# An ordering model's prices for GpSimd, crossbar transposes and weight casts, and the first batch's state scalings, in a bidirectional gated-attention block

## The chip, the cores and the metric

The kernel runs on all 8 NeuronCores of one Trainium2 chip. Each core computes 4 of the 32 sequences alone; nothing passes between cores. The metric is the device time of the slowest core, in microseconds (us). In this text PE is TensorE (matmuls), DVE is VectorE, ACT is ScalarE, POOL is GpSimd and SP is SyncE, which here issues nearly all DMAs.

## What is computed

One encoder block on x of shape (32, 2048, 1024), with 16 learned meta tokens put ahead of each sequence and dropped at the end:

```python
u = rms_norm(concat(meta, x), g_pre)
(c_b, c_c, c_x, c_z, q, k, v, r, lr_f, lr_b, m_a, m_b) = split(u @ w_in)
y_conv = c_b * conv3(c_c * c_x, conv_w) * silu(c_z)          # centred, depthwise
g_f = log_sigmoid(lr_f @ w_gate_f + b_f) / 16                # and g_b, per head and key channel
o = gla(q, k, v, g_f, j <= t) + reversed_gla(q, k, v, g_b, j > t)   # 4 heads, key 128, value 256
#   per chunk: o = mask(q_in k_in^T) v + q_in @ state ; state = state * decay + k_dec^T v
y_gla = rms_norm_per_head(o) * silu(r)
merged = sigmoid(m_a) * (y_conv @ w_out_c) + sigmoid(m_b) * (y_gla @ w_out_g)
out = x + rms_norm(merged @ w_out, g_post)
```

Inputs and output are float32; the kernel's matmuls are bf16 with float32 accumulation.

## The kernel before

A core goes through its 4 sequences ("batches" in the code, numbered 0 to 3) one after the other. For each, 16 tiles of 128 positions are normalised, transposed and kept as `uT`; then come the projections of the 4 heads (k, q, v and the gates), the chunked attention forward and backward over 16 chunks of 128 positions, the short convolution channel group by channel group, four output products done by a seven-product scheme for 2x2 blocks (`stage6`), and the last projection with norm and residual (`stage7`). All of it is written as small items in chains (`put`), each with the items it comes after.

**A list scheduler sets the order.** While the program is built, `ListScheduler.run` takes at each point the item that would keep PE waiting least, by a model: `Sched.add` gives each instruction a start (its engine free, its operands ready, 0.2 us more across engines) and an end from a booked cost, and each DMA an end from one shared transfer time of bytes / 300 GB/s plus 2 us. The model alone sets the order of the instructions on each of the five queues; on the chip every engine then runs its queue strictly in that order and waits on semaphores. A booked cost that is changed thus changes no instruction by itself, but can move any of them, in all batches.

**Booked costs.** `ecost` (line 512) prices tensor operations on POOL and DVE; `dtr` (551) is a crossbar-transposing DMA, issued on SP; the weights of batch 0 are loaded by POOL's casting DMA (float32 to bf16, line 616) and written back as bf16 to `wsc`, from which SP loads them later.

**The state scalings.** The attention's state per head is a 128 x 256 float32 tile, `TF` forward and `TB` backward. For each chunk DVE adds the chunk's product to the decayed state (`stt`, line 522, reads PSUM), and the state times the decay is written as bf16: forward into a part of `GR` (`f_P`, line 956), backward into `SB` (`b_P`, line 1000). This scaling goes through `evac`, which picks among the engines it is given the one that the model has done first. A batch has 64 forward and 60 backward ones. The backward pass of a head is 8 items `b_O`, each for two chunks: six 128 x 256 matmuls (five in the first) from `SM`, `GR` and `SB`; ahead of them stand the two `KT` products of `b_P` and the four 128 x 128 score products of `b_S`. Below, a **step** is what PE has to do from the last matmul of one `b_O` to the last of the next, seven to a head.

**What batch 0 has besides.** x tiles 8 to 15 are transposed on the crossbar, the weights are cast and written back, and POOL prepares the sums of the 2x2 scheme's weights (`prep`, 32 times: two casts and four 256-column operations, tile `OS` or `ycX`). In the profile all matmuls have line 492, all ACT work line 509; DVE and POOL tensor-tensor work is line 518, scalings and other tensor-scalar work line 527, casts and copies 536.

Of the kernel before, what the change touches and what calls it, by code (L numbers as in the profile page):

```python
# [40 lines left out]
BLK_OFF = {}  # L41
# [310 lines left out]
def build_program(NB):  # L352
    nc = bass.Bass("TRN2", target_bir_lowering=False, dynamic_dma_scratch_size=2048)

    def din(name, shape, dt=F32):
        return nc.dram_tensor(name, list(shape), dt, kind="ExternalInput").ap()
# [3 lines left out]
    w_d = din("w_all", [W_TOTAL // 256, 256])  # L360
# [65 lines left out]
    def program(S):  # L426

        G = {"st": 0, "held": ()}
# [8 lines left out]
        def free_n(ap):  # L437
            n = 1
            for d in ap.shape[1:]:
                n *= d  # L440
            return n

        def narrow(*aps):
            return all(a.dtype in (BF16, U16) for a in aps)
# [46 lines left out]
        def mm(out, lhsT, rhs, start, stop, r, w, share=1, skip=False):  # L491
            S.add("pe", lambda e: e.matmul(out, lhsT=lhsT, rhs=rhs, start=start, stop=stop, skip_group_check=skip), r, w,  # L492
                  cost=max(0.025, free_n(rhs) / 2400.0 + 0.0025) / share)
# [17 lines left out]

        def ecost(eng, n, fast):
            if eng == "pool":
                return 0.15 + 2.17e-3 * n
            return 0.15 + (0.52e-3 if fast else 1.04e-3) * n

        def tt(eng, out, a, b, op, r, w):
# [20 lines left out]
        def evac(out, in_, r, w, scale=None, engs=("act", "dve")):  # L538

            n = free_n(out)  # L540
            cost = {"act": 0.17 + 0.82e-3 * n, "dve": ecost("dve", n, narrow(out, in_)), "pool": 0.2 + 1.15e-3 * n}
            eng = min(engs, key=lambda e: max(S.free[e], S.free["pe"]) + cost[e])
            cp(eng, out, in_, r, w, scale)
# [4 lines left out]
        def dma(q, out, in_, r, w, semkey, nbytes):  # L548
            return S.add(q, lambda e: e.dma_start(out=out, in_=in_), r, w, semkey=semkey, nbytes=nbytes)  # L549

        def dtr(out, in_, r, w, semkey, nbytes):
            S.add("sp", lambda e: e.dma_start(out=out, in_=in_, transpose=True), r, w, semkey=semkey, nbytes=nbytes, hold=1.1)  # L552

        def rot(name, bufs):
            i = G.get(("rot", name), 0)
# [9 lines left out]
        def wsrc(t, blk):  # L565
            off, cols, _ = BLK_OFF[blk]
            return t[off // 256:(off + 128 * cols) // 256, :].rearrange("(p a) n -> p (a n)", p=128)

        class WPool:
# [26 lines left out]
            def load(self, n):  # L596
                blk, kind, first = self.seq[n]
                own = G["wf", self.region]
                best = None
                for i, b in enumerate(self.kinds[kind]):  # L600
                    t = [own[u] for u in self.units(b)]
                    if None not in t and (best is None or max(t) < best[0]):
                        best = (max(t), i, b)
                if best is None:
                    raise NotReady()
                _, s, b = best
                G["wf", self.region] = tuple(None if u in self.units(b) else t for u, t in enumerate(own))
                G["ws", self.name, n] = b
                ap, k = self.ap(n)
                if kind in "ab":  # L610
                    _, g, p = blk
                    lo, hi = (0, 2048) if kind == "a" else (2048, 3584)
                    dma("sp", ap, wst_d[g * 4 + p, :, lo:hi], [("wst", g, p, z, kind) for z in range(2)], k,
                        ("w", kind, s), 256 * (hi - lo))
                elif first:
                    dma("pool", ap, wsrc(w_d, blk), [], k, ("wc", self.name, s), 512 * BLK_OFF[blk][1])
                else:
                    dma("sp", ap, wsrc(wsc_d, blk), [("wsc", blk)], k, ("w", self.name, s), 256 * BLK_OFF[blk][1])

# [320 lines left out]

        def f_init(hd, b):

            i_ap, i_k = TF[1](F32)
            if b > 0:
                dma("sp", i_ap, smeta_d[hd], [("smeta", hd)], i_k, ("tf",), 1 << 17)
            G["fT"] = 1
            G["fd"] = None
# [6 lines left out]
        def f_P(H, pr, t):  # L954
            bank, bk = nps()
            for z in range(2):
                i = pr * 2 + z
                k_ap, k_k = KTf[t](BF16, (i % 4) * 128, 128)
                v_ap, v_k = H.v(i)
                mm(bank[:, z * 256:(z + 1) * 256], k_ap, v_ap, True, True, k_k + v_k, bk)  # L960
            for z in range(2):
                i = pr * 2 + z
                old, oldk = TF[G["fT"]](F32)
                new, newk = TF[1 - G["fT"]](F32)
                s_ap, s_k = H.Sf(i)
                if G["fd"] is None:
                    evac(s_ap, old, oldk, s_k, engs=("act", "pool"))
                    tt("dve", new, bank[:, z * 256:(z + 1) * 256], old, ALU.add, bk + oldk, newk)
                else:
                    dc, dk = G["fd"]  # L970
                    evac(s_ap, old, oldk + dk, s_k, scale=dc, engs=("act", "pool", "dve"))
                    stt(new, old, dc, bank[:, z * 256:(z + 1) * 256], ALU.mult, ALU.add, oldk + dk + bk, newk)
                G["fT"] = 1 - G["fT"]
                G["fd"] = (H.dc(0, i), H.dk)
# [21 lines left out]
        def b_P(H, u):  # L996
            if u == 0:
                G["bd"] = None
                G["bT"] = 0
            n1 = 7 - 2 * (u % 4)  # L1000
            bank, bk = nps()
            nz = 1 if u == 7 else 2
            for z in range(nz):
                k_ap, k_k = KTb[u % 2](BF16, (1 - z) * 128, 128)
                v_ap, v_k = H.v(n1 - z)
                mm(bank[:, z * 256:(z + 1) * 256], k_ap, v_ap, True, True, k_k + v_k, bk)
            for z in range(nz):
                old, oldk = TB[G["bT"]](F32)
                new, newk = TB[1 - G["bT"]](F32)
                if G["bd"] is None:  # L1010
                    cp("dve", new, bank[:, 0:256], bk, newk)
                else:
                    dc, dk = G["bd"]
                    stt(new, old, dc, bank[:, z * 256:(z + 1) * 256], ALU.mult, ALU.add, oldk + dk + bk, newk)
                G["bT"] = 1 - G["bT"]
                G["bd"] = (H.dc(1, n1 - z), H.dk)
                s_ap, s_k = SBs[(u * 2 + z + 1) % 5](BF16)
                dc, dk = G["bd"]
                evac(s_ap, new, newk + dk, s_k, scale=dc, engs=("act", "pool", "dve"))

        def b_O(H, u):
            n1 = 7 - 2 * (u % 4)
# [575 lines left out]
        for z in range(4):  # L1598
            ap = REG["onT"][:, 2 * z * 2048:2 * z * 2048 + 4096].rearrange("p (r t) -> p r t", r=2)[:, :, 0:1024].bitcast(F32)
            keys = onT[2 * z](BF16, 0, 1024)[1] + onT[2 * z + 1](BF16, 0, 1024)[1]  # L1600
            xnext.append((ap, keys, True))
        for z in range(2):
            ap, keys = e1(F32, z * 1024, 1024)
# [95 lines left out]
    S = Sched()  # L1699
# [105 lines left out]
```

How the kernel before makes its waits and increments, by code:

```python
    def emit(self, eng, e, sems):  # L211
        waited = {}
        for op in self.ops[eng]:
            need = {}
            for d in op.deps:
                s, v = d.sig
                if v > need.get(s, 0):
                    need[s] = v
            for s, v in need.items():
                if waited.get(s, 0) >= v:
                    continue
                e.wait_ge(sems[s], v)
                waited[s] = v
            if op.fn is None:
                continue
            ins = op.fn(e)
            if op.semkey is not None:
                ins.then_inc(sems[op.sig[0]], 16)
            elif op.need:
                ins.then_inc(sems[op.sig[0]], 1)
```

## Time and profile before

| | |
|---|---|
| three runs | 2964.33, 2966.95, 2987.33 us (median 2966.95) |
| profiled execution | 2960.34 us; span of the slowest core 2958.8 us |
| spans of the 8 cores | 2949.3 to 2958.8 us, granted clock 0.983 to 0.987 |
| busy: PE, DVE, ACT, POOL | 2811.1, 1970.0, 1547.8, 1065.0 us |

The profile is of core 3, the slowest. PE is busy for 95% of the span, so 148 us are left in which it has no matmul. The granted clock is the share of full speed that the chip allows PE; a PE that is slowed shows as longer matmuls, not as idle time.

### The profile page before, as it was taken

The page shows a single profiled execution, that of the slowest core. Times are in us where ns is not written, and L with a number is a line of the kernel's source. Part 1 is how long each engine was busy: PE and PEld are TensorE (multiplying, and loading weights), DVE is VectorE, ACT ScalarE, POOL GpSimd, SP SyncE. Part 2 cuts the span into 40 slices and gives each one's busy share as a digit, 9 for nine tenths or more (in the row PEclk, how much of TensorE's full clock was granted, in tenths as well). Part 3 has the DMA queues.
Part 4 walks back from the last instruction along what each step waited for, and adds up shares of the span by engine and source line. Part 5 has one row for each costly group of instructions (what it writes and reads, how often), then busy time and mean ns, then how long its engine had stood idle before and what let it go on. Part 6 is the DMA issues. An engine that isn't in the chain of part 4 may idle for free.

```text
span 2958.8 us, 54281 instructions; the slowest of 8 cores (2949.3 to 2958.8 us)
## 1 busy us (share of the span) xinstructions
PE 2811.1 (95%) x15740; PEld 1475.3 (50%) x15740; DVE 1970.0 (67%) x2889; ACT 1547.8 (52%) x2921; POOL 1065.0 (36%) x1447
## 2 busy tenths in 40 slices
PE   6898897999999999999999999999999999999998
PEld 4555443444456665444445665444445656544443
DVE  5556676566677786567666778557667778656665
ACT  5556664433466764443456776343346776443243
POOL 4566565232232343125143334125323234312412
PEclk9999998999999999999999999999999999999999
DMA  9997755494553223376473322349456222334445
GB/s 226 186 179 170 170 156 151 153 269 147 181 165 74 74 65 110 127 220 176 150 208 100 79 66 72 112 153 261 137 183 168 74 74 64 110 115 151 137 137 169
DMA packets 370976, 423.01 MB, mean 143 GB/s; under 512 B 220528, under 2 KB 252272, under 8 KB 370176
## 3 DMA queue, kind: packets, MB, share of 16 engines
q1 hardware_dynamic: 361760, 402.56, 47.3%
q0 software_dynamic: 8928, 16.98, 4.3%
q8 instruction: 135, 2.21, 0.3%
q14 instruction: 153, 1.25, 0.1%
HBM read 324.65 MB, written 65.60 MB: 132 GB/s over the span
## 4 chain that ended last, share of the span: by engine, by line
PE 78%; DMA 7%; SPq 4%; issue 3%; DVE 3%; POOL 3%; ACT 2%; POOLq 0%; DVEq 0%; ACTq 0%
PE ps L492 78%; SPq L552 3%; POOL sb_OS L518 1%; SPq L549 1%; DMA wsc<-sb_W 1%; DMA wst<-sb_OS 1%; DMA sb_KT<-sb_GR 1%; DMA sb_ycT<-x 1%; DMA sb_W<-wst 1%; DMA sb_uT<-sb_ycX 1%; DMA sb_onT<-sb_ON 1%; DMA sb_onT<-x 0%; DMA sb_uT<-sb_ycT 0%; DVE sb_GR L518 0%; POOL sb_ycT L518 0%
## 5 line engine op out<-in xcount | busy, mean ns | idle before, releaser
L492 PE MATMUL ps<-sb_uT,sb_W 128*128 128x512 bf16 (+3 forms) x7680 | 1608.5, 370 | 22.0 <-DMA sb_uT<-sb_ycX 7.5
L492 PEld LDWEIGHTS ps<-sb_uT,sb_W 128*128 128x128 bf16 (+1 forms) x7680 | 728.6, 98 | 780.9 <-issue 66.1
L509 ACT ACTIVATE sb_CS<-ps 128x512 f32<-128x512 f32 (+3 forms) x544 | 304.5, 569 | 285.7 <-PE ps L492 273.6
L518 POOL TENSOR_TENSOR sb_GR<-sb_CS 128x512 bf16<-128x512 f32 x128 | 166.5, 1303 | 659.8 <-DVE sb_CS L522 654.4
L492 PE MATMUL ps<-sb_GR 128*128 128x512 bf16 (+2 forms) x1792 | 350.8, 319 | 9.2 <-DVE sb_GR L518 4.1
L492 PE MATMUL ps<-sb_GR,sb_W 128*128 128x512 bf16 x1072 | 264.9, 381 | 6.7 <-ACT sb_LR L509 5.9
L522 DVE SCALAR_TENSOR_TENSOR sb_CS<-sb_CS,sb_convw 128x512 f32<-128x512 bf16 x256 | 247.2, 974 | 17.0 <-ACT sb_CS L509 6.3
L518 DVE TENSOR_TENSOR sb_CS<-ps,sb_CS 128x512 f32<-128x512 f32 (+3 forms) x288 | 181.2, 629 | 115.7 <-PE ps L492 81.0
L492 PEld LDWEIGHTS ps<-sb_GR 128*128 128x128 bf16 x1792 | 164.2, 98 | 149.4 <-issue 14.1
L492 PE MATMUL ps<-sb_W,sb_uT 128*128 128x256 bf16 x2048 | 234.9, 273 | 1.1 <-ACT sb_MT L509 0.9
L518 POOL TENSOR_TENSOR sb_CS<-sb_CS 128x512 f32<-128x512 f32 x128 | 168.2, 1317 | 167.1 <-DVE sb_CS L522 101.9
L492 PEld LDWEIGHTS ps<-sb_W,sb_uT 128*128 128x128 bf16 x2048 | 198.9, 98 | 32.3 <-issue 3.0
L699 POOL TENSOR_TENSOR sb_stat<-sb_stat,sb_cst 128x2 f32<-128x2 f32 (+2 forms) x257 | 183.0, 712 | 38.5 <-POOL sb_stat L527 0.9
L901 DVE TENSOR_TENSOR_SCAN sb_AT<-sb_smask,sb_AT 128x1024 f32<-128x1024 bf16 x64 | 149.2, 2364 | 41.5 <-ACT sb_AT L509 41.5
L527 POOL TENSOR_SCALAR sb_SB<-sb_TB,sb_dcol 128x256 bf16<-128x256 f32 x125 | 63.0, 504 | 304.7 <-DVE sb_TB L522 155.5
L492 PEld LDWEIGHTS ps<-sb_GR,sb_W 128*128 128x128 bf16 x1072 | 104.7, 98 | 135.6 <-issue 12.5
L527 POOL TENSOR_SCALAR sb_GR<-sb_TF,sb_dcol 128x256 bf16<-128x256 f32 x143 | 78.7, 551 | 252.6 <-DVE sb_TF L522 185.9
L527 POOL TENSOR_SCALAR sb_stat<-sb_stat 128x2 f32<-128x2 f32 (+2 forms) x257 | 78.4, 305 | 236.7 <-ACT sb_TB L509 143.4
L509 ACT ACTIVATE sb_SM<-ps 128x256 bf16<-128x256 f32 x384 | 144.5, 378 | 35.3 <-PE ps L492 20.3
L509 ACT ACTIVATE sb_TB<-ps 128x1024 bf16<-128x1024 f32 x64 | 65.5, 1023 | 184.3 <-PE ps L492 184.2
L522 DVE SCALAR_TENSOR_TENSOR sb_TF<-sb_TF,sb_dcol,ps 128x256 f32<-128x256 f32 x240 | 114.5, 477 | 52.2 <-DVE sb_TF L522 17.4
L509 ACT ACTIVATE sb_GR<-sb_AT 128x1024 bf16<-128x1024 f32 x128 | 133.8, 1053 | 4.1 <-DVE sb_AT L901 3.7
(155 smaller groups left out, 3749.9 us busy)
## 6 DMA issues: line engine op xcount, KB each, us to landing
sb_W<-wsc SPq DMA_DIRECT2D x272, 256.0 KB, 3.0
sb_W<-wst SPq DMA_DIRECT2D x128, 512.0 KB, 4.1
sb_W<-wst SPq DMA_DIRECT2D x128, 384.0 KB, 3.3
sb_onT<-x SPq DMA_DIRECT2D x50, 512.0 KB, 6.1
sb_GR<-x SPq DMA_DIRECT2D x40, 512.0 KB, 5.8
sb_OS<-w_pairs SPq DMA_DIRECT2D x32, 512.0 KB, 5.6
y<-sb_GR SPq DMA_DIRECT2D x32, 512.0 KB, 3.1
sb_ycT<-x SPq DMA_DIRECT2D x32, 512.0 KB, 5.8
```

The source lines that it names most:

```text
L492: S.add("pe", lambda e: e.matmul(out, lhsT=lhsT, rhs=rhs, start=start, stop=stop, skip_group_check=skip), r, w, cost=max(0.025, free_n(rhs ...
L509: S.add("act", lambda e: e.activation(out=out, in_=in_, func=func, **kw), r, w, table=TABLE.get(func), cost=0.17 + 0.82e-3 * free_n(in_) + ...
L518: S.add(eng, lambda e: e.tensor_tensor(out=out, in0=a, in1=b, op=op), r, w, cost=ecost(eng, free_n(out), narrow(out, a, b)))
L522: S.add("dve", lambda e: e.scalar_tensor_tensor(out=out, in0=in0, scalar=scalar, in1=in1, op0=op0, op1=op1), r, w, cost=0.21 + 1.05e-3 * f ...
L527: S.add(eng, lambda e: e.tensor_scalar(out=out, in0=in0, scalar1=s1, scalar2=s2, op0=op0, op1=op1), r, w, cost=c)
L549: return S.add(q, lambda e: e.dma_start(out=out, in_=in_), r, w, semkey=semkey, nbytes=nbytes)
L552: S.add("sp", lambda e: e.dma_start(out=out, in_=in_, transpose=True), r, w, semkey=semkey, nbytes=nbytes, hold=1.1)
L699: S.add("pool", lambda e: e.tensor_tensor(out=out, in0=out, in1=cst[0:np_, 0:n], op=ALU.pow), w + ["cst"], w, cost=0.6)
L901: S.add("dve", lambda e: e.tensor_tensor_scan(out=r_ap, data0=smask[:], data1=r_ap, initial=0.0, op0=ALU.mult, op1=ALU.add), e_k + ["smask ...
```

## The change

Three booked costs are changed. A POOL tensor-tensor operation of n columns is booked at 0.45 + 0.00163 n us instead of 0.15 + 0.00217 n (0.87 for 0.71 us at 256 columns, 1.28 for 1.26 at 512, 2.12 for 2.37 at 1024). A crossbar transpose is booked with twice its bytes, a casting weight load of batch 0 with 660 instead of 512 bytes a column and partition. And the engines offered to the state scalings become a variable: ACT and DVE in batch 0; ACT, DVE and POOL in the others.

```diff
         def ecost(eng, n, fast):
             if eng == "pool":
-                return 0.15 + 2.17e-3 * n
+                return 0.45 + 1.63e-3 * n
...
         def dtr(out, in_, r, w, semkey, nbytes):
-            S.add("sp", lambda e: e.dma_start(out=out, in_=in_, transpose=True), r, w, semkey=semkey, nbytes=nbytes, hold=1.1)
+            S.add("sp", lambda e: e.dma_start(out=out, in_=in_, transpose=True), r, w, semkey=semkey, nbytes=2 * nbytes, hold=1.1)
...
-                    dma("pool", ap, wsrc(w_d, blk), [], k, ("wc", self.name, s), 512 * BLK_OFF[blk][1])
+                    dma("pool", ap, wsrc(w_d, blk), [], k, ("wc", self.name, s), 660 * BLK_OFF[blk][1])
...
         def f_init(hd, b):
 
+            G["side"] = ("act", "dve", "pool") if b else ("act", "dve")
...
-                    evac(s_ap, old, oldk, s_k, engs=("act", "pool"))
+                    evac(s_ap, old, oldk, s_k, engs=G["side"])
...
-                    evac(s_ap, old, oldk + dk, s_k, scale=dc, engs=("act", "pool", "dve"))
+                    evac(s_ap, old, oldk + dk, s_k, scale=dc, engs=G["side"])
...
-                evac(s_ap, new, newk + dk, s_k, scale=dc, engs=("act", "pool", "dve"))
+                evac(s_ap, new, newk + dk, s_k, scale=dc, engs=G["side"])
```

Counted in the built programs, the 124 scalings of batch 0 are 61 on POOL, 43 on ACT and 20 on DVE before, and 66 on ACT and 58 on DVE now. (Lines after 943 are numbered two higher in the changed kernel.)

**PE, batch 0, head 3, the first step of the backward pass.** Before:

```order
L492 MATMUL ps<-sb_GR,sb_KT 128x256 x2
L492 MATMUL ps<-sb_GR 128x128 x4
L492 MATMUL ps<-sb_GR,sb_W 128x512 x4
L492 MATMUL ps<-sb_GR,sb_SM 128x256
L492 MATMUL ps<-sb_GR 128x256
L492 MATMUL ps<-sb_SB,sb_GR 128x256
L492 MATMUL ps<-sb_GR,sb_SM 128x256
L492 MATMUL ps<-sb_GR 128x256
L492 MATMUL ps<-sb_SB,sb_GR 128x256
```

And in the changed kernel (`uT,W` is projection work of the convolution and of the gate r, `GR,W` a product of stage 6):

```order
L492 MATMUL ps<-sb_uT,sb_W 128x512 x8
L492 MATMUL ps<-sb_GR,sb_KT 128x256 x2
L492 MATMUL ps<-sb_GR 128x128 x4
L492 MATMUL ps<-sb_uT,sb_W 128x512 x8
L492 MATMUL ps<-sb_GR,sb_SM 128x256
L492 MATMUL ps<-sb_GR 128x256
L492 MATMUL ps<-sb_SB,sb_GR 128x256
L492 MATMUL ps<-sb_GR,sb_SM 128x256
L492 MATMUL ps<-sb_GR 128x256
L492 MATMUL ps<-sb_SB,sb_GR 128x256
```

Sixteen 512-column matmuls from other items now stand in the step where four stood; the work of head 3's backward pass itself is the same.

**POOL before and DVE now, the same head.** POOL's row before had the scalings between the prep sums (`OS`) and the norm statistics (`stat`):

```order
L527 TENSOR_SCALAR sb_SB<-sb_TB,sb_dcol 128x256
L518 TENSOR_TENSOR sb_OS<-sb_OS 128x256 x4
L527 TENSOR_SCALAR sb_SB<-sb_TB,sb_dcol 128x256
L527 TENSOR_SCALAR sb_stat<-sb_stat 128x2
L699 TENSOR_TENSOR sb_stat<-sb_stat,sb_cst 128x2
L518 TENSOR_TENSOR sb_AT<-sb_ycT 128x1024
```

DVE's row in the changed kernel:

```order
L522 SCALAR_TENSOR_TENSOR sb_TB<-sb_TB,sb_dcol,ps 128x256
L527 TENSOR_SCALAR sb_SB<-sb_TB,sb_dcol 128x256
L522 SCALAR_TENSOR_TENSOR sb_TB<-sb_TB,sb_dcol,ps 128x256
L527 TENSOR_SCALAR sb_SB<-sb_TB,sb_dcol 128x256
L989 COPY_PREDICATED sb_SM<-sb_maskb,ps 128x256
L522 SCALAR_TENSOR_TENSOR sb_TB<-sb_TB,sb_dcol,ps 128x256
L527 TENSOR_SCALAR sb_SB<-sb_TB,sb_dcol 128x256
```

The scaling now follows the state's update on the same engine, ahead of the next update, and POOL has none.

**SP, the start of the program** (`GR<-x` loads x tiles 8 to 15, `uT<-ycX` and `uT<-ycT` transpose them in order):

```order
-L549 DMA sb_GR<-x 128x1024 x8
+L549 DMA sb_GR<-x 128x1024 x7
+L552 DMA_TRANSPOSE sb_uT<-sb_ycX 128x8x128
+L549 DMA sb_GR<-x 128x1024
 L549 DMA sb_gpost<-gpost_bc 128x1024
-L552 DMA_TRANSPOSE sb_uT<-sb_ycX 128x8x128 x2
-L552 DMA_TRANSPOSE sb_uT<-sb_ycT 128x8x128 x2
-L549 DMA wsc<-sb_W 128x1024
+L552 DMA_TRANSPOSE sb_uT<-sb_ycX 128x8x128
 L549 DMA smeta<-sb_TF 128x256
```

Tile 8 is transposed ahead of the last x load and of `gpost`; tiles 10 to 15 now come later and one by one.

## Rows read from the trace of the kernel before

**Rows 1.** page, part 1: busy time of each engine over the span.

```profile
PE 2811.1 (95%) x15740; PEld 1475.3 (50%) x15740; DVE 1970.0 (67%) x2889; ACT 1547.8 (52%) x2921; POOL 1065.0 (36%) x1447
```

**Rows 2.** stretches of the span; columns in its first line, times in us.

```profile
core 3: us, PE busy (x) PEld busy (x) DVE busy (x) ACT busy (x) POOL busy (x), PEclk, DMA share, GB/s
80.00:520.00 440.00, 379.45 (x2348) 213.74 (x2346) 283.75 (x474) 253.75 (x496) 265.16 (x362) 0.94 0.79 170
740.00:2880.00 2140.00, 2098.49 (x11716) 1103.71 (x11715) 1457.53 (x2132) 1135.58 (x2151) 676.33 (x915) 1.00 0.44 129
440.00:482.00 42.00, 25.27 (x135) 13.28 (x136) 28.28 (x55) 20.84 (x59) 23.83 (x38) 0.76 0.58 137
```

**Rows 3.** PE's waits, 80 to 520 us: total, times, longest (us).

```profile
PE ps L492 <- DMA sb_KT<-sb_GR: 13.4, 7, 3.5
PE ps L492 <- POOL sb_SB L527: 12.5, 5, 5.5
PE ps L492 <- DMA sb_W<-w_all: 6.3, 3, 4.7
PE ps L492 <- DVE sb_SM L987: 4.4, 4, 1.5
PE ps L492 <- DVE sb_GR L518: 4.1, 1, 4.1
PE ps L492 <- DVE sb_SB L527: 1.3, 1, 1.3
```

**Rows 4.** timeline of PE, the last head of batch 0: start, length (us), what.

```profile
441.09 0.27 PE L492 MATMUL ps<-sb_GR 128*128 128x128 bf16 x2 [4.12 <-DVE sb_GR L518]
441.63 1.77 PE L492 MATMUL ps<-sb_GR,sb_W 128*128 128x512 bf16 x4
463.21 0.27 PE L492 MATMUL ps<-sb_SB,sb_GR 128*128 128x256 bf16 x1
474.65 0.58 PE L492 MATMUL ps<-sb_GR,sb_KT 128*128 128x256 bf16 x2 [3.46 <-DMA sb_KT<-sb_GR]
480.85 0.37 PE L492 MATMUL ps<-sb_SB,sb_GR 128*128 128x256 bf16 x1 [1.68 <-POOL sb_SB L527]
481.08 18.18 PE L492 MATMUL ps<-sb_uT,sb_W 128*128 128x512 bf16 x72
502.56 1.03 PE L492 MATMUL ps<-sb_GR,sb_W 128*128 128x512 bf16 x4
505.14 2.75 PE L492 MATMUL ps<-sb_GR,sb_W 128*128 128x512 bf16 x12
```

**Rows 5.** state scalings to sb_SB, 0 to 740 us: ns min/median/max, first and last.

```profile
L527 POOL TENSOR_SCALAR sb_SB<-sb_TB,sb_dcol x29: 467/477/904, 147.0 to 480.0; 128x256 bf16<-128x256 f32 x29
L509 ACT ACTIVATE sb_SB<-sb_TB,sb_dcol x20: 507/508/509, 147.5 to 476.5; 128x256 bf16<-128x256 f32 x20
L527 DVE TENSOR_SCALAR sb_SB<-sb_TB,sb_dcol x11: 353/374/1282, 152.7 to 471.2; 128x256 bf16<-128x256 f32 x11
```

**Rows 6.** timeline of DVE and POOL, 277 to 279 us.

```profile
277.97 1.28 DVE L527 TENSOR_SCALAR sb_SB<-sb_TB,sb_dcol 128x256 bf16<-128x256 f32 x1
277.95 1.15 POOL L518 TENSOR_TENSOR sb_CS<-sb_CS 128x512 f32<-128x512 f32 x1
```

**Rows 7.** timeline of PE, waits for tiles, weights and transposes in batch 0.

```profile
54.32 2.44 PE L492 MATMUL ps<-sb_uT,sb_W 128*128 128x341 bf16 x8 [4.44 <-DMA sb_uT<-sb_ycX]
84.49 3.59 PE L492 MATMUL ps<-sb_uT,sb_W 128*16 128x512 bf16 x30 [3.74 <-DMA sb_uT<-sb_ycT]
227.11 5.09 PE L492 MATMUL ps<-sb_uT,sb_W 128*128 128x512 bf16 x16 [4.71 <-DMA sb_W<-w_all]
310.04 0.38 PE L492 MATMUL ps<-sb_GR,sb_KT 128*128 128x256 bf16 x2 [3.02 <-DMA sb_KT<-sb_GR]
```

**Rows 8.** PE's waits, 740 us to the end.

```profile
PE ps L492 <- ACT sb_SB L509: 11.7, 3, 4.2
PE ps L492 <- POOL sb_SB L527: 5.5, 3, 2.0
```

## The prediction

> **What bounds the kernel now.** The page's busy times come first: PE is busy for 2811.1 of 2958.8 us [rows 1], and no other engine comes near it. So only the 148 us without a matmul, and the time in which the clock is low, can be won or added to. The stretches say where they lie: in 2140 us of batches 1 to 3 PE idles for 41.5 us at a granted clock of 1.00; in the 440 us from 80 to 520, in batch 0, it idles for 60.6 us, and the clock is 0.94 [rows 2]. Batch 0 is where the gain must come from, and the later batches are where a new order could do harm three times over. Third, PE's waits in that stretch: 13.4 us for transposes into `KT`, 12.5 us for scalings on POOL, 6.3 us for cast weights, 4.4 us for `SM`, 4.1 us for a product of `GR` [rows 3]. Last, the timeline of head 3's backward pass: the last four steps, from the `SB` product at 463.21 to that at 480.85, take 17.6 us, 4.4 us each [rows 4], though each holds little work. A step is a chain through PE, DVE, a scaling and PE again. If other work does not fill it, PE waits.
>
> **Part 1: the scalings and the steps.** A 512-column matmul takes (2.75 - 1.03) / 8 = 0.215 us in a row of others [rows 4], the narrower ones in proportion. By that price I counted the PE work of each step of batch 0 in both orders. Head 3 has 1.9, 3.6, 3.7, 1.9, 1.0, 1.1 and 0.8 us before, and 4.4, 5.4, 1.9, 3.6, 4.5, 1.9 and 0.8 now. What a step lacks to 4.4 us is its shortfall. Over the four heads it sums to 3.8 + 7.3 + 3.3 + 16.8 = 31.2 us before. The waits for `KT`, `SB` and `SM` in the same stretch are 13.4 + 12.5 + 1.3 + 4.4 = 31.6 us [rows 3], so the measure fits, although a few of the `KT` waits belong to the forward pass. Now it is 4.0 + 2.2 + 5.1 + 9.4 = 20.7 us: 10.5 us less, if a step still takes 4.4 us.
>
> It need not. A scaling leaves POOL, where the median is 477 ns, for ACT at 508 ns or DVE at 374 ns [rows 5]; by duration that is no matter. But DVE also does the state's updates, in order. It gets 34 - 11 = 23 backward scalings more over 28 steps, about 0.31 us a step. In head 3 DVE is busy for 28.3 of 42 us [rows 2], so some 67% of that, 0.2 us, lies on the path: 4.6 us a step, at which the new order lacks 24.2 us. **I take -7.0 us** (bounds -10.5, with no lengthening, and +21.3, the rival below). The 61 scalings taken from POOL free some 30 us there; POOL does not bound this stretch (265 of 440 us, rows 2 show it), so I cost that at nothing: what hides it is PE's own work.
>
> DVE's scaling has a worse side. At 277.97 us one took 1.28 us, and POOL had begun a 1.15 us multiplication at 277.95 [rows 6]; their ends lie 0.15 us apart. The range 353 to 1282 ns on 11 scalings [rows 5] shows that this happens, and the median that it is not the rule. The Trainium skill, "SBUF — State Buffer", section "Who interferes with whom", says that VectorE and GpSimd share a pair of ports as an exclusive lock, and that a `tensor_scalar` in a two-port mode and a GpSimd operation block each other for a whole instruction. That pair of rows agrees; by this rule the sum would be that of the second rival.
>
> **Part 2: the wait ahead of head 3.** PE stands still for 4.12 us at 441.09 until DVE has made the gated queries [rows 4]. In the new order those score products come 15 us of PE work earlier, with the usual projection groups ahead of them, and the multiplication that they need has moved on DVE too; which of the two moved more no row can show. **-1 us** (bounds -4.1, all of it, and +4.1, as much again).
>
> **Part 3: transposes and casts booked longer.** Twice the bytes is 0.44 us more for 128 KB and 0.87 us for 256 KB at the model's 300 GB/s, so the model puts what needs them later. In the trace the forward products wait 3.02 us at 310.04 for `KT`, and 4.71 us at 227.11 for cast weights [rows 7]. Only a part can go: a step moved in the queue carries its DMA issue along, and SP's row has other transposes in it. **-3 us** (bounds -9, nearly all of 6.3 and 3.0, and +3, one more wait like that at 310.04).
>
> At the start PE waits 4.44 us for tile 8 and 3.74 us for tile 15 [rows 7]. Tile 8 is now issued before an x load and `gpost`, which shortens the first. Tiles 10 to 15 are issued later, behind `smeta` and write-backs, and whole-tile projections of the second half have moved back by only some 4 us of PE work. What is late next is tile 15. **0 us** (bounds -6 and +6).
>
> **Part 4: the clock.** From 440 to 482 us the granted clock is 0.76 [rows 2], between its two levels of 1.2 and 2.4 GHz. The 72 matmuls behind it take 18.18 us [rows 4] instead of 72 x 0.215 = 15.5, so 2.7 us of work is lost after some 20 us of idling; with shorter matmuls within the stretch I put it at 0.2 us for each us of idling. For -11 us that gives **-2 us** (bounds 0 and -6).
>
> **Part 5: batches 1 to 3.** The steps move there too, through the two new prices. PE's waits for `SB` are 11.7 + 5.5 = 17.2 us there [rows 8], above all in one step with 1.0 us of work in each batch. In the new order no step there has under 2.5 us of work, but more of them have 2.5 to 3. Counted to 4.4 us, the shortfall goes from 13.6 to 17.4 us a batch, which would cost 11.4 us. But that measure would also have PE wait 40 us there before, where it waits for `SB` 17, so it is too strict and long steps near 3 us mostly pass. **-2 us** (bounds -15 and +11).
>
> **Sum:** -7 - 1 - 3 + 0 - 2 - 2 = -15 us against the profiled execution's 2960.3: 2945.3. The three runs shown are 2964.3, 2967.0 and 2987.3, so the two quick ones lie 4 and 6.6 us above the profiled one; I add 4: **2949 us**, 0.6% below the median shown.
>
> **The rivals.**
> - *All the mispriced waits go* (chance 0.18). Steps stay at 4.4 us (-10.5), the wait at 441 (-4.1), tile 8's (-4.4), the forward transposes and casts (-9) vanish, the clock gives 0.2 x 28 = 5.6, and the step with 1.0 us of work is gone in the later batches (-8): -41.6, or 2923 us with the same 4 added. For it: each is a wait in the rows. Against: an order that closes one gap takes the filling work from somewhere else.
> - *DVE becomes what a step waits for* (0.14), the slower end. Place: the backward steps of batch 0. A DVE scaling that meets a POOL operation takes 1.28 instead of 0.37 us [rows 6], and POOL, which no longer waits for DVE's states, has its prep sums and multiplications running more of the time. With 1.6 us more a step, 6.0, the new order lacks 52.5 us: +21.3, the clock +4, and nothing gained in parts 2 and 3: 2960.3 + 25.3 + 4 = 2990 us, and 2997 with two thirds of part 5's worst. It decides from 5.0 us a step: there the new shortfall reaches the old 31.2.
> - *A wash* (0.18). Work that fills head 3 is missing before it: the new order reaches head 3's first `SB` product with 8.5 us less PE work done, and heads 1 and 2 begin 17 and 28 us of PE work earlier, with their weights and tiles needed earlier. If the waits reappear there: 2964 us, within 6.
> - That the change does not do what it says can be excluded for the scalings: the order has none on POOL in batch 0.
>
> The forecast itself has 0.50, with its own range of 2934 to 2963.
>
> **The numbers.** A measurement of this kernel can tell about 1% from no change, 2937 and 2997 us. Faster by more: the first rival nearly whole (0.16) and the forecast's lower edge (0.05): 0.21. Slower by more: a third of the second rival (0.05) and a little for what no row shows: 0.06. Within: 0.73. The range leaves out half of the first rival (0.09) and most of the second (0.1): **2922 to 2980 us**.
>
> **What would show it.** In the changed profile the stretch from 80 to 520 us should idle some 50 instead of 61 us, and waits for `SB` on POOL should be gone from it. Head 3's backward pass should have a granted clock over 0.85, and its steps 4.4 to 4.8 us where they have little work. Part 1 is wrong if DVE's scalings have a mean over 0.8 us or PE waits over 15 us for DVE's `SB` and `SM` in batch 0. Part 3 is wrong if the waits for `KT` and `w_all` keep their 20 us together. Part 5 is wrong if batches 1 to 3 idle over 50 or under 35 us in 2140. The forecast as a whole falls if batch 0's idling stays and the time still changes, since then the later batches decide.

## The result, and the profile after

The changed kernel takes **2940.94 us** (median; the kernel before 2977.14 beside it), a ratio of **0.9898, 95% interval 0.985 to 0.9946**: 1.0% faster, where 0.6% and 2949 us were forecast. Both medians are of four runs; runs in which the cores of a die are slowed, one of each four here, are left out of all ratios, and x4 is not in the table below because its profiled run was one. The profiled execution takes 2938.5 us (2960.3 before), and its slowest core is now core 6, not core 3.

The page's busy times, for [rows 1]:

```profile
PE 2799.3 (95%) x15502; PEld 1480.5 (50%) x15740; DVE 1984.0 (68%) x2905; ACT 1593.3 (54%) x2973; POOL 1069.0 (36%) x1405
```

PE is still the bound. The stretches of [rows 2], now on core 6:

```profile
core 6: us, PE busy (x) PEld busy (x) DVE busy (x) ACT busy (x) POOL busy (x), PEclk, DMA share, GB/s
80.00:520.00 440.00, 398.09 (x2363) 224.69 (x2392) 298.25 (x514) 261.15 (x518) 256.16 (x322) 0.89 0.80 175
740.00:2880.00 2140.00, 2092.82 (x11596) 1107.78 (x11776) 1468.39 (x2130) 1183.30 (x2195) 699.26 (x931) 1.00 0.45 130
440.00:482.00 42.00, 32.05 (x170) 16.92 (x171) 33.37 (x67) 21.29 (x60) 22.21 (x34) 0.83 0.59 151
```

In batch 0 PE idles for 42 us of 440 instead of 61, but on this core at a granted clock of 0.89 instead of 0.94. (PE's count in the second row is some 180 below PEld's; those matmul records are missing, so 47 us of idling are too many.)

PE's waits from 80 to 520 us, total, times and longest, for [rows 3]:

```profile
PE ps L492 <- ACT sb_SB L509: 13.4, 3, 9.7
PE ps L492 <- DMA sb_KT<-sb_GR: 10.8, 5, 6.4
PE ps L492 <- ACT sb_W L509: 3.7, 1, 3.7
PE ps L492 <- DVE sb_SM L989: 3.1, 3, 1.5
```

The waits for `SB` on POOL, for cast weights and for the gated queries are gone on this core, as forecast. Waits for `SB` on ACT of the same size have come, 9.7 us of them in one piece. The state scalings, for [rows 5] (ns min/median/max):

```profile
L527 DVE TENSOR_SCALAR sb_SB<-sb_TB,sb_dcol x34: 352/353/1349, 166.9 to 476.1; 128x256 bf16<-128x256 f32 x34
L509 ACT ACTIVATE sb_SB<-sb_TB,sb_dcol x26: 497/508/512, 166.3 to 479.1; 128x256 bf16<-128x256 f32 x26
```

DVE does 34 instead of 11, none the slower in the median; 7 of the 34 took over 0.4 us, and the mean is 0.43. Head 3's backward pass, for [rows 4]:

```profile
450.51 0.30 PE L492 MATMUL ps<-sb_SB,sb_GR 128*128 128x256 bf16 x1 [3.14 <-ACT sb_SB L509]
...
473.08 1.86 PE L492 MATMUL ps<-sb_ycT,sb_W 128*128 128x512 bf16 x4 [3.68 <-ACT sb_W L509]
...
479.71 0.37 PE L492 MATMUL ps<-sb_SB,sb_GR 128*128 128x256 bf16 x1 [0.55 <-ACT sb_SB L509]
480.52 15.85 PE L492 MATMUL ps<-sb_uT,sb_W 128*128 128x512 bf16 x62 [0.44 <-DVE sb_onT L518]
```

The projections behind it run at 0.256 us each, as before (18.18 / 72 = 0.253): the clock has not come back there on this core. The 9.7 us wait, in the timeline of all engines:

```profile
218.10 0.31 PE L492 MATMUL ps<-sb_GR 128*128 128x256 bf16 x1
...
219.50 4.95 DVE L901 TENSOR_TENSOR_SCAN sb_AT<-sb_smask,sb_AT 128x1024 f32<-128x1024 bf16 x2 [3.54 <-ACT sb_AT L509]
219.53 5.44 POOL L518 TENSOR_TENSOR sb_OS<-sb_OS 128x256 f32<-128x256 f32 x2
...
226.88 0.47 DVE L522 SCALAR_TENSOR_TENSOR sb_TB<-sb_TB,sb_dcol,ps 128x256 f32<-128x256 f32 x1
...
227.45 0.51 ACT L509 ACTIVATE sb_SB<-sb_TB,sb_dcol 128x256 bf16<-128x256 f32 x1 [0.47 <-DVE sb_TB L522]
...
228.10 0.37 PE L492 MATMUL ps<-sb_SB,sb_GR 128*128 128x256 bf16 x1 [9.69 <-ACT sb_SB L509]
```

DVE's row has two gate scans, which wait for ACT, and four forward updates ahead of the backward update that PE needs. Nothing is wrong with the scaling; it comes last in a queue.

**Where the time went, stage by stage.** One measure serves for all kernels below. PE's work up to a given matmul is counted from the order at 2400 columns per us (0.213 us for 512 columns; the rows give 0.215). The *excess* of a stretch is its time less that work: idling and slow clock together. The landmarks are the first and last `SB` product of batch 0, the first of batch 1, the last of batch 3, and the end. Means over the 8 cores, us, one profiled execution each:

| kernel | to first SB | batch 0's backward steps | to batch 1's first SB | batches 1 to 3 | end | sum |
|---|---|---|---|---|---|---|
| before | 36.5 | 74.7 | 14.1 | 44.9 | 21.9 | 192 |
| **changed** | 44.5 | 56.9 | 4.8 | 35.7 | 22.1 | 164 |
| x1 engines only | 44.0 | 87.5 | 11.2 | 56.5 | 23.6 | 223 |
| x2 prices only | 41.5 | 57.8 | 15.7 | 38.9 | 22.3 | 176 |
| x3 changed, POOL 0.46 | 44.7 | 73.0 | 4.5 | 37.2 | 22.0 | 181 |
| x8 crossbar price only | 36.8 | 83.8 | 2.9 | 52.6 | 27.8 | 204 |
| x9 changed, cast 700 | 47.8 | 59.2 | 16.1 | 36.4 | 22.3 | 182 |
| x10 changed, cast 745 | 42.3 | 69.2 | 7.2 | 36.7 | 22.1 | 178 |
| x6 changed, scalings on POOL | 45.5 | 56.0 | 6.8 | 36.3 | 22.6 | 167 |
| x7 before, scalings off POOL | 36.6 | 77.5 | 14.7 | 45.2 | 21.6 | 196 |
| x5 changed, state first | 44.8 | 53.4 | 5.9 | 37.9 | 22.9 | 165 |
| x11 before, casts on POOL | 38.2 | 78.5 | 8.4 | 43.8 | 21.3 | 190 |
| x12 changed, both edits | 49.4 | 57.6 | 7.3 | 40.3 | 22.2 | 177 |

So the mean core gained 28 us (the slowest 22): 19 come from batch 0 and 9 from the later batches. The runs of one order differ too (x12's from 2943.7 to 2962.1 us, and its profile is the longest of them): sums less than 10 us apart decide nothing by themselves.

Nor were the rows taken side by side. The kernel before took 2969.8 us in the mean beside x1 to x4, 2966.3 beside x5 to x8, 2980.5 beside x9 and x10 and 2976.0 beside x11 and x12, and its row in the table is of a quick execution, 2960.3 us. By the ratios x9 to x12 lie 23, 32, 10 and 22 us under the kernel before, by these sums only 10, 14, 2 and 15. Where the two differ, the ratio counts, since its two kernels ran together.

The later batches can be read on core 3, which has the same 7731 matmuls between the last `SB` products of batches 1 and 3 in both kernels. Before, and then now:

```profile
1142.30:2550.90 1408.60, 1381.54 (x7731) 727.78 (x7729) 968.96 (x1413) 754.19 (x1431) 455.92 (x619) 1.00 0.46 133
```

```profile
1137.10:2539.70 1402.60, 1376.68 (x7731) 726.38 (x7728) 968.83 (x1403) 782.26 (x1452) 467.22 (x627) 1.00 0.46 134
```

It is 6.0 us less, 4.9 of it shorter matmuls. PE's waits from 740 us on, for [rows 8]:

```profile
PE ps L492 <- POOL sb_SB L527: 9.6, 7, 1.8
PE ps L492 <- DVE sb_CS L518: 5.5, 3, 1.8
```

The three waits for `SB` on ACT of up to 4.2 us are gone; seven on POOL of up to 1.8 us stand in their place. In slices of 100 us the granted clock before fell to 0.97 or 0.98 in three of the 14 slices of this stretch on core 3; now it is 1.00 in all.

### The profile page after: what moved, and what is told of

It reads as the page before. It is cut to its first block, busy times and chain, and to the rows that moved or that the text cites. A ratio compares the mean times of both kernels' runs of the same rounds, so it can differ in the third digit from the quotient of the medians.

```text
span 2936.9 us, 53943 instructions; the slowest of 8 cores (2916.5 to 2936.9 us)
## 1 busy us (share of the span) xinstructions
PE 2799.3 (95%) x15502; PEld 1480.5 (50%) x15740; DVE 1984.0 (68%) x2905; ACT 1593.3 (54%) x2973; POOL 1069.0 (36%) x1405
## 3 DMA queue, kind: packets, MB, share of 16 engines
q1 hardware_dynamic: 361760, 402.56, 47.8%
## 4 chain that ended last, share of the span: by engine, by line
PE 82%; DVE 4%; DMA 4%; issue 3%; SPq 3%; ACT 2%; POOL 1%; DVEq 0%; POOLq 0%; ACTq 0%
PE ps L492 82%; SPq L552 2%; DMA sb_KT<-sb_GR 1%; SPq L549 1%; DVE sb_CS L522 1%; DMA sb_W<-wst 1%; DMA sb_onT<-x 1%; DVE sb_GR L518 1%; DMA wst<-sb_OS 1%; DMA sb_W<-wsc 1%; ACT sb_CS L509 0%; DVE sb_AT L518 0%; DVE sb_CS L518 0%; DVE sb_TF L522 0%; DMA sb_uT<-sb_ycT 0%
## 5 line engine op out<-in xcount | busy, mean ns | idle before, releaser
L492 PE MATMUL ps<-sb_uT,sb_W 128*128 128x512 bf16 (+3 forms) x7518 | 1585.1, 369 | 25.8 <-DVE sb_CS L518 5.5
L492 PE MATMUL ps<-sb_W,sb_uT 128*128 128x256 bf16 x2048 | 243.6, 278 | 0.0
L509 ACT ACT_TABLE_LOAD x112 | 143.7, 1283 | 37.5 <-PE ps L492 24.8
L527 POOL TENSOR_SCALAR sb_GR<-sb_TF,sb_dcol 128x256 bf16<-128x256 f32 x108 | 61.6, 571 | 217.3 <-DVE sb_TF L522 200.4
```

The source lines that it names most:

```text
L509: S.add("act", lambda e: e.activation(out=out, in_=in_, func=func, **kw), r, w, table=TABLE.get(func), cost=0.17 + 0.82e-3 * free_n(in_) + ...
L527: S.add(eng, lambda e: e.tensor_scalar(out=out, in0=in0, scalar1=s1, scalar2=s2, op0=op0, op1=op1), r, w, cost=c)
```

## The experiments

### Each half alone: x1, x2

x1 has the engines of the change and the prices of before, x2 the prices of the change and the engines of before. Against the kernel before, x1 and then x2:

```diff
+            G["side"] = ("act", "dve", "pool") if b else ("act", "dve")
...
-                    evac(s_ap, old, oldk, s_k, engs=("act", "pool"))
+                    evac(s_ap, old, oldk, s_k, engs=G["side"])
...
-                    evac(s_ap, old, oldk + dk, s_k, scale=dc, engs=("act", "pool", "dve"))
+                    evac(s_ap, old, oldk + dk, s_k, scale=dc, engs=G["side"])
...
-                evac(s_ap, new, newk + dk, s_k, scale=dc, engs=("act", "pool", "dve"))
+                evac(s_ap, new, newk + dk, s_k, scale=dc, engs=G["side"])
```

```diff
-                return 0.15 + 2.17e-3 * n
+                return 0.45 + 1.63e-3 * n
...
-            S.add("sp", lambda e: e.dma_start(out=out, in_=in_, transpose=True), r, w, semkey=semkey, nbytes=nbytes, hold=1.1)
+            S.add("sp", lambda e: e.dma_start(out=out, in_=in_, transpose=True), r, w, semkey=semkey, nbytes=2 * nbytes, hold=1.1)
...
-                    dma("pool", ap, wsrc(w_d, blk), [], k, ("wc", self.name, s), 512 * BLK_OFF[blk][1])
+                    dma("pool", ap, wsrc(w_d, blk), [], k, ("wc", self.name, s), 660 * BLK_OFF[blk][1])
```

> Only the engines of batch 0's state scalings are changed; the three prices are those of before. Counted at 4.4 us a step the order lacks 49.2 us of PE work in batch 0's backward steps (before 31.3, the change 20.5), and 21.4, 13.4, 13.4 in batches 1 to 3. Theory STEPS (what the steps lack of work sets the loss): slower than before by 5 to 20 us, with batch 0 some 10 us worse than before. Rival PRICES (better prices make orders that the chip can follow; the engines matter little): within 5 us of before. Rival RE-PLANNING (any new order is a fresh draw, and this change drew a good one): no sign foreseen, 5 to 15 us either way.

> Only the three prices are changed; the scalings of batch 0 may go to POOL as before. The order lacks 32.7 us in batch 0's backward steps (before 31.3) and 17.4 us in each later batch (13.4). STEPS: batch 0 loses what it lost before, within 4 us; in all -3 to +8 us against before. PRICES: most of the gain of the whole change, -15 to -28 us, and the later batches' excess as in the changed kernel (16, 12, 12 us a batch, mean over the cores). RE-PLANNING: no sign foreseen.

Measured: x1 0.7% slower than before (1.0074, 1.0045 to 1.0103), x2 0.5% faster (0.9947, 0.9926 to 0.9968). The halves do not add up: +22 and -16 us alone, -30 together. x1 went as STEPS has it, at a little over its 20 us. Its waits on core 3 from 80 to 520 us, against [rows 3]:

```profile
PE ps L492 <- DMA sb_KT<-sb_GR: 21.8, 6, 5.4
PE ps L492 <- ACT sb_SB L509: 16.1, 11, 5.5
```

Without POOL, and with the old prices, `SB` is waited for longer than with it. x2 speaks against STEPS (-3 to +8 us) and lies in PRICES' range, -15 to -28: its steps lack as much work as before (32.7 to 31.3 us), and their excess is 17 us less. The later batches gain with x2 alone, 6 of the 9 us; the last 1945 rows of PE's order are the same in x2, x3 and the change.

### One price moved by a hair: x3, x4

x3 against the changed kernel, and x4 against the kernel before:

```diff
-                return 0.45 + 1.63e-3 * n
+                return 0.46 + 1.63e-3 * n
```

```diff
-                return 0.15 + 2.17e-3 * n
+                return 0.16 + 2.17e-3 * n
```

> The changed kernel with one price moved by 0.01 us: a POOL tensor-tensor operation is booked at 0.46 + 0.00163 n instead of 0.45 + 0.00163 n. No chip duration fits one better than the other. The order lacks 36.3 us in batch 0's backward steps instead of 20.5, and 17.4 in each later batch as in the change. STEPS: batch 0 loses 8 to 14 us of what it gained; 2949 to 2955 us where the change has 2941. PRICES: as the change, within 4 us. RE-PLANNING: differs from the change by 5 to 15 us, most likely slower, since the change is the better of two draws.

> The kernel before with one price moved by 0.01 us: a POOL tensor-tensor operation is booked at 0.16 + 0.00217 n instead of 0.15 + 0.00217 n. The order lacks 33.1 us in batch 0's backward steps (before 31.3) and 13.4 in each later batch (13.4). STEPS: as before, within 4 us. PRICES: as before, within 4 us. RE-PLANNING: 5 to 15 us either way; if the kernel before was an unlucky draw, faster.

Measured: x3 0.9955 (0.9939 to 0.9971) of the time before, so over half of the gain is lost to 0.01 us in one price (the intervals of x3 and of the change just meet, at 0.994 to 0.995). All of that is in batch 0's backward steps (56.9 to 73.0 us); the later batches keep theirs. x4 1.0007 (0.9994 to 1.002): no difference. Both are as STEPS has it, x3 at a little more than its price; x3 is as RE-PLANNING has it too, and x4 as PRICES has it and not as RE-PLANNING.

### The engine or the order: x6, x7

These move instructions in the built queues, once the kernel has been planned, and plan nothing anew; PE's and SP's rows stay word for word. `shift` gives a scaling to another engine and puts it into that engine's row by its planned start. x6 does so in the changed kernel, x7 in the kernel before:

```diff
+    side = sorted((op for e in ("act", "dve") for op in S.ops[e] if op.side), key=lambda op: op.t0)
+    for op in side[::2]:
+        shift(S, op, "pool")
...
```

```diff
+    side = [op for op in S.ops["pool"] if op.side]
+    for i, op in enumerate(side):
+        shift(S, op, ("dve", "act")[i % 2])
...
```

> The changed kernel; every second scaling of batch 0 is taken from ACT or DVE and put on POOL, into POOL's row by the model's start time; PE, SP and all other rows keep their order. Theory ENGINE (a scaling on POOL waits behind prep sums and statistics, and PE for it): 8 to 20 us slower than the change, with 8 us or more of PE waits for SB on POOL in batch 0. Rival ORDER (the work between the steps makes the gain, whichever engine scales): within 5 us of the change.

> The kernel before; the scalings that POOL has in batch 0 are put on DVE and ACT in turn, into their rows by the model's start time; PE, SP and all other rows keep their order. ENGINE: the 10.3 us (mean over the cores) that PE waits for SB on POOL in batch 0 go, 8 to 13 us faster than before. ORDER: the steps are as empty as before and wait for SB on DVE or ACT instead; within 4 us of before.

Measured: x6 0.9903 (0.9868 to 0.9938) of before, the same as the change; x7 1.0019 (0.9999 to 1.0038), the same as before. **At a fixed order it makes no difference which engine does the scalings.** x6 has some 60 of them on POOL in batch 0, as the kernel before has. x6's waits on core 2, and then x7's on core 6, 80 to 520 us:

```profile
PE ps L517 <- POOL sb_SB L574: 11.0, 4, 10.1
...
PE ps L517 <- ACT sb_SB L534: 6.3, 4, 3.4
```

```profile
PE ps L517 <- DVE sb_SB L573: 9.3, 4, 4.1
...
PE ps L517 <- ACT sb_SB L572: 3.5, 3, 2.4
```

The waits keep their size and change the name of the engine. In x6 the 10.1 us wait is now "for POOL", behind the same scans. ENGINE falls: its 8 us of waits on POOL came in x6, and the time did not. Of ORDER it is shown that the order decides and not the engine; that it does so by the work between the steps is not shown by these two.

### The crossbar price alone: x8

Against the kernel before:

```diff
-            S.add("sp", lambda e: e.dma_start(out=out, in_=in_, transpose=True), r, w, semkey=semkey, nbytes=nbytes, hold=1.1)
+            S.add("sp", lambda e: e.dma_start(out=out, in_=in_, transpose=True), r, w, semkey=semkey, nbytes=2 * nbytes, hold=1.1)
```

> Only the crossbar transposes are booked with twice their bytes; all else is as before. The order lacks 38.9 us in batch 0's backward steps (before 31.3) and 17.6 us in each later batch. PRICES: the later batches gain what they gained with all three prices, 5 to 9 us over batches 1 to 3 (the 11.7 us of waits for SB on ACT gone), and batch 0's waits for KT shrink; 8 to 16 us faster than before. STEPS: batch 0 is 5 to 10 us worse, the sum within 5 us of before. RE-PLANNING: no sign foreseen for batch 0.

Measured: 1.0054 (1.0039 to 1.0068), slower. Batch 0's steps lose 9 us as STEPS has it (38.9 for 31.3 us), the later batches 8 and the end 6; only the stretch behind the steps gains, 11. PRICES, in the form that this price makes the later gain, falls. So does STEPS' sum: 16 us slower, not within 5. x1 (engines) and x8 make the later batches worse, and x9 and x10 (cast price) hardly move them. That points to the POOL price for their gain, alone or with the crossbar's, but it was not run by itself.

### The measure put to the test: x9, x10

x9 against the changed kernel; x10 has 745 in the same place:

```diff
-                    dma("pool", ap, wsrc(w_d, blk), [], k, ("wc", self.name, s), 660 * BLK_OFF[blk][1])
+                    dma("pool", ap, wsrc(w_d, blk), [], k, ("wc", self.name, s), 700 * BLK_OFF[blk][1])
```

> The changed kernel with the cast weight loads booked at 700 instead of 660 bytes a column and partition. Of 34 orders built with this price between 550 and 860, the order lacks 17.8 to 40.4 us of PE work in batch 0's backward steps (mean 29.5; before 31.3, the change 20.5); this one has the least, 17.8. The order of batches 1 to 3 is that of the change but for a few rows. Over the six planned orders measured so far PE's idle time between the first and the last SB product of batch 0 (mean over the cores) goes as 15 us + 0.85 x shortfall (32.1 us in the change, 48.0 before). STEPS: 30 us idle there, and 2932 to 2944 us, as the change. Rival PRICE (660 fits the chip best, and a price further off makes it worse): 5 to 15 us slower than the change. RE-PLANNING without any measure: no number foreseen for either of these two kernels.

> The changed kernel with the cast weight loads booked at 745 instead of 660 bytes a column and partition: of those 34 orders the one that lacks most in batch 0's backward steps, 40.4 us, twice the change's 20.5. Batches 1 to 3 as in the change. STEPS: 50 us idle between the first and the last SB product of batch 0 where the change has 32.1, and 12 to 22 us slower than the change (2953 to 2963). PRICE: like x9, 5 to 15 us slower than the change, and no further from x9 than 5 us, since 700 and 745 are nearly the same price.

Measured: x9 0.9921 (0.9883 to 0.9959), x10 0.9893 (0.9839 to 0.9947) of before, which the ratios cannot tell from each other or from the change. PE idles in the backward steps for 38.0 and 44.5 us where 30 and 50 were expected: the right way round, at a third of the distance. Over the eight planned orders shortfall and idling go together with a correlation of 0.79, so the measure says something of the steps. But x9 loses 11 us behind them and 3 ahead, which the measure doesn't see, and the sums of x9 and x10 lie 4 us apart. As a forecast of the time it failed. PRICE does not fit either: 745 is no worse than 700. The profiles of all three neighbours of the change (x3, x9, x10) have 14 to 18 us more excess, 12 to 17 of it in batch 0. Only x3's ratio bears that out: x9 and x10 ran beside a kernel before that took some 11 us more than beside x3, and by their ratios they keep most or all of the gain.

### The longest new wait taken away: x5

In the changed kernel, once it has been planned, the update at 226.88 (`tb`) and its scaling at 227.45 (`side`) go ahead of the two scans at 219.50 in DVE's row:

```diff
...
+    dve.remove(tb)
+    S.ops["act"].remove(side)
+    side.eng, side.fn = "dve", side.alt["dve"]
+    dve[scan:scan] = [tb, side]
...
```

> The changed kernel with two instructions moved and nothing planned anew: on DVE the state update into TB that PE waits for at 218 to 228 us, and its scaling (on ACT before, now on DVE right behind it), stand ahead of the two gate scans. All other instructions keep their order on all queues. Theory WAIT AND CLOCK: the 9.7 us wait goes on every core, and with it the low clock that cores 6 and 7 keep from 200 to 320 us (0.71, 0.81, 0.85) and that makes core 6 the slowest; 2922 to 2932 us where the change has 2941, with the spread of batch 0 between the cores down from 23 to under 12 us. Rival DEFERRED: the scans end no earlier, so PE meets the same wait one or two steps later; 2937 to 2943 us.

Measured: no ratio; the profiled execution took 2935.39 us (the change 2938.5). The wait is gone and the clock of core 6 did recover, first the changed kernel, then x5:

```profile
200.00:240.00 40.00, 28.18 (x179) 18.27 (x179) 28.53 (x54) 21.56 (x47) 25.08 (x31) 0.71 0.72 161
240.00:280.00 40.00, 39.74 (x220) 22.32 (x221) 28.95 (x52) 25.09 (x56) 22.98 (x32) 0.81 0.79 182
280.00:320.00 40.00, 38.88 (x234) 22.03 (x235) 25.02 (x48) 25.09 (x46) 19.92 (x30) 0.86 0.99 172
```

```profile
200.00:240.00 40.00, 29.76 (x176) 17.76 (x179) 29.46 (x45) 22.92 (x49) 27.74 (x30) 0.83 0.75 180
240.00:280.00 40.00, 37.60 (x275) 24.56 (x276) 29.23 (x61) 26.95 (x63) 27.02 (x42) 1.00 0.81 182
280.00:320.00 40.00, 30.99 (x205) 17.98 (x205) 19.96 (x45) 22.96 (x43) 11.98 (x21) 0.87 1.00 187
```

PE is busy for 39.7 and 37.6 us in the middle rows, with 220 matmuls at 0.81 and 275 at 1.00. Then x5 idles 9 us in the next row, and its waits on this core say for what:

```profile
PE ps L508 <- DMA sb_KT<-sb_GR: 14.5, 5, 8.9
PE ps L508 <- ACT sb_SB L525: 4.4, 2, 3.4
```

`SB` on ACT fell by 9.0 us and `KT` rose by 3.7, with `MT`, `TF` and `GR` behind it. Core 6 gains 11 us in batch 0, the mean of the cores 3, the whole nothing that can be told. The spread of batch 0 between the cores falls from 24 to 17 us, not under 12. DEFERRED is nearer.

### ACT held by a cast: x11, x12

The wait of 3.0 us ahead of a `ycT` product in the kernel before is an instance of something wider. ACT and PE there, in the timeline:

```profile
524.61 0.63 ACT L509 ACTIVATE sb_OS<-sb_OS 128x512 bf16<-128x512 f32 x1 [4.65 <-POOL sb_OS L518]
525.15 0.58 ACT L509 ACTIVATE sb_W<-ps 128x512 f32<-128x512 f32 x1
```

```profile
525.87 1.02 PE L492 MATMUL ps<-sb_ycT,sb_W 128*128 128x512 bf16 x4 [3.00 <-ACT sb_W L509]
```

The last cast of a weight preparation (`ops` in `prep`) waits on ACT for POOL's sums, and the copy that frees PE's bank stands behind it. From 80 to 560 us ACT waits 75.7 us like this before and 36.7 in the change (means over the cores). POOL's sums in that stretch, before and now (busy, mean ns):

```profile
L518 POOL TENSOR_TENSOR sb_OS<-sb_OS 128x256 f32<-128x256 f32 (+1 forms) x106 | 100.1, 944 | 12.4 <-POOL sb_OS L518 1.2
```

```profile
L518 POOL TENSOR_TENSOR sb_OS<-sb_OS 128x256 f32<-128x256 f32 (+1 forms) x110 | 98.0, 891 | 12.7 <-POOL sb_OS L518 0.4 <-ACT sb_ycX L509 0.2
```

The new price of 0.87 us fits the mean where 0.71 did not. The same sums, before and now, by ns min/median/max:

```profile
L518 POOL TENSOR_TENSOR sb_OS<-sb_OS x106: 712/727/2701, 81.4 to 524.7; 128x256 f32<-128x256 f32 x62, 128x256 bf16<-128x256 f32 x44
```

```profile
L518 POOL TENSOR_TENSOR sb_OS<-sb_OS x110: 713/726/2780, 84.2 to 492.6; 128x256 f32<-128x256 f32 x64, 128x256 bf16<-128x256 f32 x46
```

The old price of 0.71 fits the median. What lifts the mean are few: on core 6 now, seven sums that began while DVE ran a scan took 2.52 to 2.78 us each. Still, the better mean looked like the cause of batch 0's gain. So the last casts were put on POOL, right behind their sums, at a fixed order: in x11 in the kernel before, in x12 in the changed one, together with x5's edit.

```diff
...
+    for op in [op for op in S.ops["act"] if op.side == "prep"]:
+        S.ops["act"].remove(op)
+        op.eng, op.fn = "pool", op.alt["pool"]
+        at = max(pool.index(d) for d in op.deps if d in pool)
+        pool.insert(at + 1, op)
...
```

> The kernel before; the last cast of each weight preparation in batch 0, which ACT does 27 times and for which it stands still until POOL's four sums are done, is put on POOL right behind those sums (27 x 0.7 us more for POOL). PE, DVE and SP keep their rows. From 80 to 560 us ACT waits 75.7 us (mean over the cores) for POOL's sums before, and 36.7 us in the change; its own queue, with scalings, evacuations and copies that PE waits for, stands behind that. Theory BLOCKED ACT: this is the common cause of much of batch 0's loss, and booking the sums right (0.87 for 0.71 us, measured 0.89) is what halved it; 6 to 15 us faster than before. Rival ORDER: PE waits where its steps lack work, whatever holds ACT; within 4 us of before.

> The changed kernel with both edits at a fixed order: the state update of 218 us and its scaling ahead of the two gate scans on DVE (as in x5), and the 30 casts that ACT does for the weight preparation put on POOL behind their sums. BLOCKED ACT: the 3.9 us of waits for ACT's copies into W and some of the 4.7 us for SB on ACT that x5 left go, and the clock with them; 2922 to 2932 us, faster than both kernels. ORDER / DEFERRED: the waits come back as waits for KT and cast weights; 2933 to 2941.

Measured: x11 0.9965 (0.9935 to 0.9995), x12 0.9926 (0.99 to 0.9952) of before. ACT's waits for sums are 0 in both. In x11 that removes what it should behind the steps: from 480 to 560 us on core 3 PE waited before

```profile
PE ps L492 <- ACT sb_W L509: 4.9, 2, 3.0
```

and not at all now, and the stretch to batch 1's first `SB` goes from 14.1 to 8.4 us. But the steps take 3.8 us more, with `KT` waits at 17.1 for 11.4 us. The whole gain is 0.35%, 10 us: that is in BLOCKED ACT's 6 to 15, but the interval (1.5 to 19 us) holds ORDER's 4 as well. x12 beats the kernel before and not the change; its 2944 to 2962 us are over both forecasts. On its slowest core:

```profile
PE ps L514 <- DMA sb_KT<-sb_GR: 24.5, 7, 14.4
PE ps L514 <- DMA sb_W<-w_all: 15.4, 3, 5.6
```

The casting loads of weights are issued from POOL's queue, and 30 casts have been put ahead of them; that this delays them is argued from the queue and was not tested. x6 speaks against BLOCKED ACT from the other side: there ACT's waits for sums rise from 36.7 to 65.3 us, and the time stays. BLOCKED ACT is shown for the waits behind head 3. That it made the gain in the steps is not: x6 has ACT nearly as blocked as before and keeps the gain.

## Why the prediction was right, and where not

**The outcome** lay in the range and in the likeliest case: 1.0% faster, 22 us by the profiled executions where 15 were summed. The sum came right through terms that were not, and that is luck.

**Part 1 (-7).** PE's idling between the first and last `SB` product of batch 0 went from 48.0 to 32.1 us (mean). That is over twice the term, but most of it is not in the waits that the term was built on. Those for `KT`, `SB` and `SM` went from 26.8 to 22.1 us there (31.6 to 27.3 in the rows of the two slowest cores), and those for `SB` alone did not fall: 12.2 to 13.9. The rest is the gated queries (4.0 to 0.3), cast weights (3.8 to 0.6), which parts 2 and 3 price, and the forward state in `TF` and `GR` (7.2 to 1.1), for which no term stood. A step's length is no constant either: the three of head 3 with under 2 us of work took 2.1, 7.9 and 3.5 us in the mean, where the prediction's test wanted 4.4 to 4.8. The count of work between the steps goes with the gain across orders, loosely. That the engine is "by duration no matter" held more strictly than meant (x6, x7). The test that the prediction set was too weak: waits for `SB` on POOL did vanish (10.9 us), and 13.6 us on ACT came.

**Part 2 (-1)** was nearly all of it, some 4 us, the lower bound. **Part 3 (-3):** `KT` and cast weights together cost 10.8 us instead of 19.7 in the stretch, which is right in kind and three times the term. At the start the step failed: "what is late next is tile 15" was wrong, the first `KT` transpose is. PE waits 7.1 us for it on core 6; all waits for `KT` ahead of the first `SB` product went from 1.4 to 9.9 us in the mean:

```profile
PE ps L492 <- DMA sb_KT<-sb_GR: 7.1, 1, 7.1
```

The excess up to there rose by 8.0 us, where 0 was summed and 6 was the bound.

**Part 4 (-2).** The idling in the steps fell by 16 us and PE's lengthening there by 1.9 (excess less idling, 26.7 to 24.8), not by the 3 that 0.2 us for each us gives. Head 3 has 0.83 on core 6 and not over 0.85.

**Part 5 (-2) came to -9.** Its measure gave +11 and was rightly distrusted; what went is the 1.0-us step of each batch, which the first rival priced at -8. Idling showed little of that (27.6 to 24.4 us over two batches, mean of the six cores with all records); the larger part is PE time, 4.9 of 6.0 us on core 3. The test on idling, 35 to 50 us, could not see it.

**No term at all** stood for the stretch behind head 3, where 9.3 us went. x11 shows that 5.7 us of such waits hang on ACT held by casts.

**The rivals.** DVE did not become the bound: PE waits 3.1 us for `SM` and hardly for DVE's `SB`. The Trainium skill, "SBUF — State Buffer", section "Who interferes with whom", names an exclusive lock for a `tensor_scalar` in a two-port mode. With a median of 353 ns, 7 of 34 over 0.4 us and a largest of 1349 ns, the DVE scalings were held too seldom here to matter. A wash (2964 us, within 6) did not come, and not in the neighbours of the change either: the slowest of them, x3, is at 0.9955 of before.

**What stays open:** what in an order decides batch 0's excess. Five edits at a fixed order moved the sum by 1 to 13 us in the profiles; the eight planned orders lie between 164 and 223. How much of batch 0's 19 us another price would have kept is open too: x3 keeps 3 by its sum, x9 and x10 more by their ratios than by theirs. Nor was it tried why `KT` comes late when ACT or DVE is freed.

## What to carry to other kernels

Where a model plans all queues, a changed price or engine is a new draw of the whole order: time two or three neighbouring values as well, and credit the edit only with what they all show (here 0.45% by the ratios, with 6 to 9 us in the later batches, and not the whole of the 19 in batch 0). Time the kernel before beside each of them: it moved by up to 14 us between sittings. To learn whether an edit itself does anything, move the instructions in the finished order and plan nothing anew. A wait that is removed in a chain of many queues must be looked for one step further on, and count slow matmuls with the idling.

## What the runs showed of the hardware

- Two DVE scans that began at 219.50 took 4.95 us, and two POOL sums that began at 219.53 took 5.44 us, where a sum takes 0.73 in the median and 0.89 in the mean. POOL was held for about as long as the scans ran: the seven sums that began during a scan from 80 to 560 us took 2.52 to 2.78 us each. The Trainium skill, "SBUF — State Buffer", section "Who interferes with whom", says that a DVE instruction with two SBUF inputs contends with a GpSimd one that reads SBUF; the rows agree, and a price for such a sum depends on what DVE does beside it.
- After the same 9.7 us wait six cores had a granted clock of 1.00 from 240 to 280 us; cores 6 and 7 had 0.81 there and 0.85 to 0.86 until 320 us. Nothing in the rows says why these two.
